# The first column tile of a head's r unit, moved ahead of the head's output matmuls

## The reference

```python
def gla_output(o, r, w):
    B, T = r.shape[:2]
    return rmsnorm(o, w).reshape(B, T, GLA_V_W) * jax.nn.silu(r)
...
    g_f = gla_log_decay(glr_f, gw_f, gb_f)      # log_sigmoid(lowrank @ w + b) / 16
    o_f, _ = gla_chunk_scan(qg, kg, vg, g_f, s_f)
    o_b, _ = gla_chunk_scan(flip_time(qg), flip_time(kg), flip_time(vg), flip_time(g_b), s_b)
    y_gla = gla_output(o_f + flip_time(o_b), gr, gla_norm_w)
```

## Time and profile before

| what | us |
|---|---|
| median of 3 runs | 2439.12 (2439.02 to 2442.89) |
| the profiled execution, its own time | 2435.55 |
| its span | 2433.7 |
| TensorE busy in the span | 2306.6 |
| VectorE busy | 1365.4 |
| ScalarE busy | 886.6 |
| GpSimd busy | 169.9 |

### The profile page before, as it was taken

The page is one execution under the profiler, slowest core; times in us unless marked ns, Lnnn a source line. Parts: engine busy times, 40 slices in busy tenths (PEclk is TensorE's granted clock), DMA queues, the critical chain, the costliest instruction groups (busy, mean ns, idle before and its releaser), DMA issues.

```text
span 2433.7 us, 29354 instructions
## 1 busy us (share of the span) xinstructions
PE 2306.6 (95%) x12273; PEld 1947.7 (80%) x12273; DVE 1365.4 (56%) x1780; ACT 886.6 (36%) x1280; POOL 169.9 (7%) x253
## 2 busy tenths in 40 slices
PE   6999999998799999999999999999999889989998
PEld 4888887876688887878888878888878778889998
DVE  4778723466356454476663268786246646556554
ACT  3222212454434354242222142222134635455442
POOL 0000000000133331000000000000000023230000
PEclk8999999999999999999999999999999999999999
DMA  8566522221212221345552336574223133325663
GB/s 288 182 207 196 170 101 87 69 71 35 70 53 69 70 70 52 104 130 170 167 173 87 104 94 205 180 228 151 93 87 105 53 96 96 104 87 153 185 184 137
DMA packets 298251, 302.05 MB, mean 124 GB/s; under 512 B 7392, under 2 KB 268488, under 8 KB 297096
## 3 DMA queue, kind: packets, MB, share of 16 engines
q1 hardware_dynamic: 297696, 300.00, 39.3%
q10 hardware_dynamic: 424, 0.18, 0.0%
HBM read 299.10 MB, written 1.05 MB: 123 GB/s over the span
## 4 chain that ended last, share of the span: by engine, by line
PE 86%; DVE 7%; ACT 3%; issue 2%; DMA 1%; SPq 1%; POOL 0%; DVEq 0%; ACTq 0%
PE PS L1363 25%; PE PS L1364 24%; PE PS L1365 24%; DVE WL L900 2%; PE PS L1746 1%; PE PS L1501 1%; PE PS L1805 1%; PE PS L1440 1%; PE PS L1442 1%; PE PS L1441 1%; PE PS L1757 1%; ACT WH L556 1%; PE PS L1643 1%; PE PS L1699 1%; PE PS L1467 1%
## 5 line engine op out<-in xcount | busy, mean ns | idle before, releaser
L1363 PE MATMUL PS<-hH,WH 128*128 128x512 f32 (+1 forms) x2096 | 766.4, 366 | 19.3 <-DVE hL L969 15.1
L1364 PE MATMUL PS<-hL,WH 128*128 128x512 f32 (+1 forms) x2096 | 754.7, 360 | 0.0
L1365 PE MATMUL PS<-hH,WL 128*128 128x512 f32 (+1 forms) x2096 | 754.0, 360 | 0.0
L900 DVE TENSOR_TENSOR WL<-raw,WH 128x1024 fp32r<-128x1024 f32 x420 | 503.1, 1238 | 440.9 <-ACT WH L556 440.5
L556 ACT CAST WH<-raw 128x1024 fp32r<-128x1024 f32 x420 | 419.5, 1047 | 400.4 <-PE PS L1365 386.6
L1363 PEld LDWEIGHTS PS<-hH,WH 128*128 128x128 f32 x2096 | 401.0, 191 | 93.8 <-issue 30.4
L1365 PEld LDWEIGHTS PS<-hH,WL 128*128 128x128 f32 x2096 | 400.5, 191 | 59.4
L1364 PEld LDWEIGHTS PS<-hL,WH 128*128 128x128 f32 x2096 | 401.0, 191 | 57.0 <-issue 1.2
L925 DVE SCALAR_TENSOR_TENSOR mraw<-mraw,cst 128x1024 f32<-128x1024 f32 x224 | 274.1, 1278 | 18.0 <-DMA mraw<-in_w_mod 17.9
L1363 PE MATMUL PS<-hidH,WH 128*128 128x512 f32 (+1 forms) x704 | 261.3, 371 | 0.0
L1364 PE MATMUL PS<-hidL,WH 128*128 128x512 f32 (+1 forms) x704 | 255.3, 363 | 0.0
(11 more groups left out here) (197 smaller groups left out, 2674.9 us busy)
## 6 DMA issues: line engine op xcount, KB each, us to landing
raw<-in_ffn_w SPq DMA_DIRECT2D x176, 512.0 KB, 5.2
mraw<-in_w_mod SPq DMA_DIRECT2D x128, 512.0 KB, 4.6
raw<-in_w_in SPq DMA_DIRECT2D x54, 1024.0 KB, 5.2
raw<-in_ffn_w SPq DMA_DIRECT2D x44, 1024.0 KB, 4.9
raw<-in_w_branch_attn SPq DMA_DIRECT2D x8, 1024.0 KB, 5.2
raw<-in_w_branch_gla SPq DMA_DIRECT2D x8, 1024.0 KB, 5.1
raw<-in_w_out SPq DMA_DIRECT2D x8, 1024.0 KB, 5.1
mfirst_b<-in_w_mod SPq DMA_DIRECT2D x4, 1024.0 KB, 10.2
```

Source lines behind the costliest of these rows:

```text
L900: nc.vector.tensor_tensor(half(WL, n % 2, e, rows), half(raw, n % 2, e, rows), half(WH, n % 2, e, rows).bitcast(F32), ALU.subtract).then_i ...
L1363: mm(o, wh, ah, start=start, stop=False)
L1364: mm(o, wh, al, start=False, stop=False)
L1365: return mm(o, wl, ah, start=False, stop=stop)
```

## The change

In `gla_head` the first column tile of the r unit, with the wait for its PSUM bank, goes ahead of the waits of the output matmuls. The second stays behind the next head's logits. Nothing else is edited, on no other engine. The number of instructions is the same.

```diff
@@ -1789,6 +1789,8 @@
                     if k + 1 in at:
                         at[k + 1]()
 
+                evicted(2)
+                tile_cols(n + 3, 0, 2, hH, hL, T)
                 pe.wait_ge(lv_acc, 7 * q + 7)
                 pe.wait_ge(lv_prod, c + 9)
                 pe.wait_ge(st_step, 6 * q + 6)
@@ -1806,9 +1808,8 @@
                 ins.then_inc(o_done, 1)
                 if h < GH - 1:
                     logits(l, h + 1)
-                for e in range(2):
-                    evicted(2 + e)
-                    tile_cols(n + 3, e, 2 + e, hH, hL, T)
+                evicted(3)
+                tile_cols(n + 3, 1, 3, hH, hL, T)
                 turn(l, h)
```

## The result

The changed kernel takes 2453.85 us, median of 4 runs (2452.9 to 2456.4), against 2439.07 for the kernel before (2438.1 to 2442.9): ratio 1.0056, interval 1.0043 to 1.0070, that is 14.8 us more. The forecast was 2447.0, the range 2441 to 2452. The sign was right. The size was not, and the time lies outside the range.

The account below looks back on a forecast made before the run. The prediction took TensorE's queue to bound the kernel, with outputs waiting for nothing. Four added waits of hats, 1.5 + 2.1 + 1.6 + 2.7 = 7.9 us, on the median 2439.12 gave 2447.0 us, range 2441 to 2452.

Parts of the forecast that it names:

- What bounds it; the outputs wait for nothing: TensorE is 86% of the chain; output matmuls start 0.23 us after the last branch matmul, their last keep done 1.8 us earlier.
- Turn holds, by 0.3 us at the tightest: Head 3 of layer 1: norm one tile later ends at 2172.2, `turn` starts at 2172.48; cost taken as 0.
- Which heads pay: Delay reaches hats only where the next head follows at once: heads 0 to 1 and 2 to 3 of each layer.
- The four waits: Added waits of hats: 1.5 and 2.1 us in layer 0, 1.6 and 2.7 in layer 1, 7.9 in all.
- head 1 of layer 0: Added hats wait of 1.5 us: low bound 0.3, plus 1.1 for VectorE's split meeting GpSimd; high bound 1.7.
- Head 3 of layer 0: Added hats wait of 2.1 us, cover already gone; low bound 1.6, or 2.6 with VectorE meeting GpSimd.
- Does the lost time come back: Level 3 waits behind hats might swallow the delay; they move along, so recovery costed at 0, other end the whole sum.
- The clock: Lower-clock spells after TensorE's waits, about 1.7 us each, may come or go; 0 for the mean, 3 us either way.
- spells: Rival: each of the four new waits is followed by 1.4 us of lower clock; 13.5 us in all, 2452.6, chance 0.10.

Follow-up runs that it names:

- odd_heads: Kernel before with the tile moved only in heads 1 and 3 of each layer; 2439.06 us, ratio 1.0000.
- even_heads: Kernel before with the tile moved only in heads 0 and 2 of each layer; 2452.33 us, ratio 1.0055.
- Pool_held: Changed kernel, with GpSimd's level 1 differences held until the product for hats is done in heads 1 and 3 of layer 0; 2455.03 us, ratio 1.0055.
- layer0: Kernel before with the tile moved in layer 0 alone; 2446.49 us, ratio 1.0024.
- filled: Changed kernel with throwaway transposes of the identity in the four places where hats newly waits; 2446.92 us, ratio 1.0028.

## Why the prediction was wrong in size

- **What bounds it; the outputs wait for nothing**: right. L1807 has no wait, and odd_heads, where only this could show, is at 1.0000.
- **Turn holds, by 0.3 us at the tightest**: right, L1708 has no wait. The norm there ended at 2189.92 + 0.88 = 2190.80, against `turn` at 2191.16.
- **Which heads pay**: right. Only those that the next head follows at once, by odd_heads and even_heads.
- **The four waits**: 8.4 us against a sum of 7.9. Three terms held (for head 1 of layer 0 luck helped a little: 0.3 + 1.1 is 1.4, I took 1.5, and 1.54 was measured). Head 3 of layer 0 was mis-sized at 2.1; it was 3.05 (3.59 - 0.54). I had let one VectorE instruction group meet GpSimd there. Three did, all of those between the gated product and hats: 2.36, 3.19 and 1.64 us where they took 1.29, 2.36 and 1.22 before, 2.3 us more in all. Pool_held gives 1.7 us of that wait back. My high bound for it, 2.6, was too low too.
- **Does the lost time come back**: I took 0. The waits of levels 2 and 3 in head 1 gave 0.3 back (0.27 + 2.36 for 2.92), in the changed kernel, even_heads, layer0 and filled alike. Small.
- **The clock**: this is the step that failed. I took 0 for the mean and 3 either way, on the ground that moved heads may gain or lose a spell alike. But the change doesn't only move stops of TensorE, it adds four, each of them followed within 17 us by a level 3 wait of 2.4 to 2.9. What the clock took on top of the 8.4 us of waits is 11.7 - 8.4 = 3.3 us in even_heads and 14.8 - 8.4 = 6.4 in the changed kernel, with the same waits in both; 3.7 us of it lie behind hats of head 3, layer 1, in the profiles of both. Filling the four waits with work takes 5.4 us off even_heads. I had priced this as the rival *spells*, 13.5 us and a chance of 0.10; with 2452.6 it was the nearest. The evidence against it that I used, one wait with no spell behind it, was one draw in one profile: behind the same wait odd_heads has a spell.
- What stays uncertain is the size, not the step. The medians give 11.7 and 14.8 us for the same waits, and the interval of the changed kernel's ratio reaches from 10.5 to 17 us. That the first two profiles differ by 20.8 us is scatter on top: layer 1's attention alone accounts for 9, and odd_heads is as slow there without a cost in the median.

## What to carry to other kernels

Before moving work ahead of a wait, look whether the trace shows the wait; here it was absent, and the only effect was to delay what hung on the outputs. On an engine whose clock falls with idleness, count a new stop as its length plus a lower-clock spell of the size that the trace shows behind other stops. Look first at the stops that are already there, since here taking 16.4 us of them away brought 23.6. Take the cost of a stop from several profiles, or from medians, since one profile can show or miss a spell by chance. When a wait can't be removed, throwaway matmuls in its place are a cheap test of what the clock takes; here they could have been left in, at 13.2 us less.

## What the runs showed of the hardware that was not expected

- Useless work made the kernel faster: 38 us of transposes in ten waits of 2.5 to 9 us, 13.2 us off the time, with the GLA stretches at 0.99 and 1.00 of full clock for 0.97 and 0.96.
- The waits of hats and of the levels are the same to 0.02 us from execution to execution, and the spells at the lower clock are not: layer 1's attention had 0.97 in one profile of the kernel before, 0.94 in another, and 0.92 in odd_heads, whose waits are the same.
- A VectorE split of two 128 x 1024 halves with both inputs in SBUF took 2.35 us alone and 3.19 to 3.54 beside GpSimd's subtractions, and the 128 x 1024 product 1.22 against 1.64. The Trainium skill (SBUF — State Buffer, Who interferes with whom) says that a VectorE instruction with two SBUF inputs contends with a GpSimd instruction that reads SBUF. The trace agrees, by these durations and by pool_held. The sizes are from here, and the lines are from the changed kernel, head 1 of layer 0:

```profile
733.89 3.54 DVE L900 TENSOR_TENSOR WL<-raw,WH 128x1024 fp32r<-128x1024 f32 x2
737.34 1.63 DVE L1207 TENSOR_TENSOR dq<-dq,gkq 128x1024 f32<-128x1024 f32 x1
```
